# Splitting a tile's expert queries between two rounds, gathering its retrieval into fewer ticks, and gate rows by transposing a column

## What is computed

```python
for l in range(DEPTH):                                    # 2
    mod = silu(c) @ ada_w[l] + ada_b[l]                   # 6 sections of 1024
    sh_m, sc_m, g_m, sh_f, sc_f, g_f = split(mod, 6)
    h = rmsnorm(x, norm_mix_g[l]) * (1 + sc_m) + sh_m
    cols = h @ w_in[l]                                    # 1024 x 3332
    y = concat(diff_attention(cols), rwkv7(cols), forgetting_attention(cols))
    x = x + g_m * (y @ w_out[l])
    h = rmsnorm(x, norm_ffn_g[l]) * (1 + sc_f) + sh_f
    q = (h @ wq).reshape(tokens, 8 heads, 2, 128)
    s = q . subkeys                                       # 2 x 128 scores a head
    # top 16 of each half, top 16 of their 256 sums -> 16 experts of 16384 a head
    u, v = u_tab[eidx], v_tab[eidx]                       # 128 experts a token
    coef = softmax(top scores) * gelu(u . h)
    x = x + g_f * sum(coef * v)
out = rmsnorm(x, final_norm_g)
```

## Time and profile before

| | us |
|---|---|
| median of 3 runs (1898.29 to 1904.04) | 1902.0 |
| the profiled execution | 1903.03 |
| its span | 1901.2 |
| lead, to the first expert row | 290.75 |
| round 0, round 1, round 2, round 3 | 425.35, 421.2, 422.4, 325.0 |
| after the last tick | 16.5 |

### The profile page before, as it was taken

The page is one execution under the profiler, slowest core; times in us unless marked ns, Lnnn a source line. Parts: engine busy times, 40 slices in busy tenths (PEclk is TensorE's granted clock), DMA queues, the critical chain, the costliest instruction groups (busy, mean ns, idle before and its releaser), DMA issues.

```text
span 1901.2 us, 20926 instructions
## 1 busy us (share of the span) xinstructions
PE 1616.6 (85%) x6868; PEld 1006.0 (53%) x6868; DVE 1394.7 (73%) x3315; ACT 673.4 (35%) x1640; POOL 515.2 (27%) x564
## 2 busy tenths in 40 slices
PE   1767678898999998898999998898999997887776
PEld 1656665554665655564665655554665652332222
DVE  5866598997856758998765748988765759985554
ACT  1313114334732334335632235325632233331112
POOL 2000013222233232222233232222232233343331
PEclk9889788998999999998999999999999998999999
DMA  9982688997799999998999999998899999999996
GB/s 393 422 346 101 242 353 348 367 421 286 283 399 421 422 420 395 363 422 313 321 403 421 421 421 399 370 402 293 287 403 421 421 415 401 416 407 421 421 421 256
DMA packets 96989, 706.08 MB, mean 371 GB/s; under 512 B 10992, under 2 KB 11504, under 8 KB 13296
## 3 DMA queue, kind: packets, MB, share of 16 engines
q0 software_dynamic: 80640, 587.24, 77.1%
q1 hardware_dynamic: 16240, 117.50, 15.1%
HBM read 703.64 MB, written 1.05 MB: 371 GB/s over the span
## 4 chain that ended last, share of the span: by engine, by line
PE 49%; DVE 28%; DMA 16%; ACT 3%; issue 3%; POOL 0%; DVEq 0%; ACTq 0%; POOLq 0%
PE psum L772 26%; DMA ringmem<-in_peer_uv_dram,eidx 11%; DVE ringmem L1435 9%; PE psum L648 5%; PE psum L412 4%; DMA W<-in_w_groups_dram 3%; PE psum L635 2%; DMA ringmem<-in_ada_pairs_dram 2%; PE psum L520 1%; PE psum L508 1%; DVE ringmem L1079 1%; PE psum L518 1%; PE psum L415 1%; DVE coef L1448 1%; ACT diag L1050 1%
## 5 line engine op out<-in xcount | busy, mean ns | idle before, releaser
L772 PE MATMUL psum<-ringmem,diag 128*128 128x512 f32 x2048 | 978.4, 624 | 132.3 <-ACT diag L1050 132.0
L379 POOL DMA_INDIRECT ringmem<-in_peer_uv_dram,eidx x512 | 489.5, 956 | 1131.5 <-PE psum L772 1079.7
L1435 DVE SCALAR_TENSOR_TENSOR ringmem<-ringmem,psum 128x1024 f32<-128x1024 f32 x512 | 612.5, 1220 | 195.3 <-DMA ringmem<-in_peer_uv_dram,eidx 180.1
L772 PEld LDWEIGHTS psum<-ringmem,diag 128*128 128x128 f32 x2048 | 389.1, 199 | 608.1 <-issue 409.1
L1050 ACT ACTIVATE diag<-K,coef 128x128 f32<-128x128 f32 x512 | 176.4, 393 | 225.8 <-DVE coef L1448 225.6
L412 PE MATMUL psum<-hT,W 128*128 128x128 f32 x1344 | 172.3, 287 | 40.9 <-DMA W<-in_w_groups_dram 19.1
L412 PEld LDWEIGHTS psum<-hT,W 128*128 128x128 f32 x1344 | 169.2, 203 | 64.9 <-issue 38.0
L1042 ACT ACTIVATE coef<-dots 128x2 f32<-128x2 f32 x256 | 51.8, 202 | 408.6 <-DVE ringmem L1435 407.7
L1079 DVE SCALAR_TENSOR_TENSOR ringmem<-ringmem,diag 128x1024 f32<-128x1024 f32 x96 | 115.3, 1223 | 20.9 <-DMA ringmem<-in_ada_pairs_dram 18.8
L648 PEld LDWEIGHTS psum<-hT,W 128*128 128x128 f32 x1024 | 123.2, 197 | 12.8 <-issue 7.2
L648 PE MATMUL psum<-hT,W 128*128 128x128 f32 x1024 | 126.0, 281 | 3.1 <-ACT hT L821 3.0
(11 more groups left out here) (243 smaller groups left out, 1629.7 us busy)
## 6 DMA issues: line engine op xcount, KB each, us to landing
ringmem<-in_ada_pairs_dram POOLq DMA_DIRECT2D x48, 1024.0 KB, 19.0
W<-in_w_pieces_dram SPq DMA_DIRECT2D x48, 1024.0 KB, 9.2
W<-in_w_groups_dram SPq DMA_DIRECT2D x24, 1536.0 KB, 11.3
W<-in_w_groups_dram SPq DMA_DIRECT2D x12, 1024.0 KB, 9.6
ringmem<-in_peer_uv_dram,eidx POOLq DMA_INDIRECT x512, 11.7
W<-in_w_groups_dram SPq DMA_DIRECT2D x4, 1040.0 KB, 9.2
attn<-in_subkeys_t_dram SPq DMA_DIRECT2D x4, 1024.0 KB, 9.5
K<-in_consts_dram SPq DMA_DIRECT2D x1, 1546.0 KB, 18.1
```

The source lines that it names most:

```text
L379: nc.gpsimd.indirect_dma_start(slot(k), None, rows, bass.IndirectOffsetOnAxis(ap=eidx[:, ph % 2, m:m + 1], axis=0)).then_inc(row_landed[q ...
L772: mm = nc.tensor.matmul(acc[:, q], diag[:, k % DIAGS, :], slot(k)[:, D:][:, q], start=(k % SEL == 0), stop=(k % SEL == SEL - 1), skip_grou ...
L1435: ins = v.scalar_tensor_tensor(out=u, in0=u, scalar=1.0, in1=hrep, op0=ALU.mult, op1=ALU.mult, accum_out=dots[:, j:j + 1])
```

## The change

1. **The split of the queries.** The lead ends after segment 64 (`LEAD_END`), when the queries of heads 0 to 3 are done and heads 0 and 1 are found; segments 65 to 78 of mixing 0 run in the first ticks of round 0. In rounds 0 to 2 the next tile's mixing goes up to segment 70 (`MIX_END`), and its segments 71 to 78 (query of head 7, scores of heads 6 and 7) run in the first ticks of the round that follows. The next tile's mixing starts in tick 7 of round 0 and in tick 3 of rounds 1 and 2, where it was tick 1.
2. **Retrieval.** Segments 61 to 64 do two parts each instead of 61 to 68 one each. Heads 2 to 7 are found in ticks 1 to 16 (`FIND`), by turns two parts and one part a tick, where it was one part in each of ticks 0 to 23.
3. **`lead_pace`.** Pieces of `ada` per segment: 1.15 up to 28 (was 1.3), 0.9 up to 56 (was 0.5 up to 50, then 1.6), 3 up to 64.
4. **Gate rows.** TensorE transposes a column of `MC` that is read 128 times; the diagonals on ScalarE and the product with ones are gone. The row of `g_f` is made in segment 58 instead of 75 and 76.

```diff
-def pace():
-
-    total, done, out = sum(COST), 0, [-1] * TICKS
-    for n, w in enumerate(COST):
-        tick = 1 + (TICKS - 3) * done // total
-        for m in range(tick, TICKS):
-            out[m] = n
+LEAD_END, MIX_END = 65, 71
+
+
+def pace(ph):
+
+
+    first = MIX_END if ph else LEAD_END
+    todo = [(n, -1) for n in range(first, SEGMENTS)]
+    if ph + 1 < PHASES:
+        todo += [(END - 1, n) for n in range(MIX_END)]
+    else:
+        todo += [(END - 1, n) for n in (4, 6, 75, 76, 77)]
+    cost = [COST[old if new < 0 else new] for old, new in todo]
+    done, total, out = 0, max(sum(cost), 1100), [(first - 1, -1)] * TICKS
+    for (old, new), w in zip(todo, cost):
+        for m in range((TICKS - 4) * done // total, TICKS):
+            out[m] = (old, new)
         done += w
     return out
...
-    for seg in range(2, SEGMENTS):
-        due += 1.3 if seg <= 28 else 0.5 if seg <= 50 else 1.6
+    for seg in range(2, LEAD_END):
+        due += 1.15 if seg <= 28 else 0.9 if seg <= 56 else 3
         out += [seg] * (int(min(due, ADA_CHUNKS)) - len(out))
-    return out + [SEGMENTS] * (ADA_CHUNKS - len(out))
...
+FIND = [[] for _ in range(TICKS)]
+for _n in range(4 * (PH - 2)):
+    FIND[1 + 2 * _n // 3].append((2 + _n // 4, _n % 4))
...
+                        if i and seg == QRY0 + 1:
+
+                            for half in range(2):
+                                gate_row(g_at(i, 2 + half), (i - 1) // NT, G_F, half, bank[4 + half],
+                                         ("hT_dve", at("hT_dve", i, 3)))
...
-                        if i and seg == 75:
-                            gate_row(g_at(i, 2), gdiag[1], bank[6], ("q_sb", at("q_sb", i, 7)))
-                        elif i and seg == 76:
-                            gate_row(g_at(i, 3), gdiag[1], bank[6], ("g_sb", g_at(i, 3)))
-
-                def gate_row(nth, src, dst, bank_free):
-
-                    pe.wait_ge(s["g_diag"], nth + 1)
+
+                def gate_row(nth, l, section, half, dst, bank_free):
+
+                    pe.wait_ge(s["mod_ready"], 3 if l else 2)
                     pe.wait_ge(s[bank_free[0]], bank_free[1])
                     for j in range(4):
-                        mm = nc.tensor.matmul(dst[:, j * P:(j + 1) * P], ones[:], src[:, j, :], start=True, stop=True)
-                    mm.then_inc(s["g_out"], 1)
+                        k = 4 * half + j
+                        tr = nc.tensor.transpose(dst[:, j * P:(j + 1) * P],
+                                                 MC[:, l, section, k:k + 1].broadcast_to([P, P]), ident)
+                    tr.then_inc(s["g_out"], 1)
...
-                Pace(mixing(0)).upto(END - 1)
+                own = Pace(mixing(0))
+                own.upto(LEAD_END - 1)
                 place_h(0)
                 for ph in range(PHASES):
                     beside = Pace(mixing(ph + 1) if ph + 1 < PHASES else last_gate())
                     for m in range(TICKS):
-                        beside.upto(PACE[m])
+                        own.upto(PACE[ph][m][0])
+                        beside.upto(PACE[ph][m][1])
                         if m == TICKS - 1 and ph + 1 < PHASES:
                             place_h(ph + 1)
                         weigh(ph * TICKS + m)
+                    own = beside
...
-                        elif 61 <= seg <= 68:
-                            retrieve(i, (seg - 61) // 4, (seg - 61) % 4)
+                        elif 61 <= seg <= 64:
+                            for part in range(2):
+                                retrieve(i, (seg - 61) // 2, 2 * ((seg - 61) % 2) + part)
...
-                        if m < 4 * (PH - 2):
-                            retrieve(ph, 2 + m // 4, m % 4)
-                        beside.upto(PACE[m])
+                        for h, part in FIND[m]:
+                            retrieve(ph, h, part)
+                        own.upto(PACE[ph][m][0])
                         if m == 0 and ph:
                             add_sum(ph - 1)
+                        beside.upto(PACE[ph][m][1])
                         coefficients(n)
+                    own = beside
```

More of the change, by code:

```diff
@@ L150, in trunk @@
     gelu, exp, sig = ACT.Gelu, ACT.Exp, ACT.Sigmoid
-    PACE, LEAD = pace(), lead_pace()
+    PACE, LEAD = [pace(ph) for ph in range(PHASES)], lead_pace()
     with ExitStack() as ctx:
@@ L791, in gate_exp @@
                     nc.scalar.activation(e, e, exp, accum_out=gsum[:, i % 2, h:h + 1]).then_inc(s["gate_exp"], 1)
-                def gate_diag(l, section, half, dst):
-                    for j in range(4):
-                        ins = nc.scalar.activation(dst[:, j, :], ident, ACT.Copy,
-                                                   scale=MC[:, l, section, 4 * half + j:4 * half + j + 1])
-                    ins.then_inc(s["g_diag"], 1)
                 def gate_copy(nth, half, src):
```

62 lines of the change are left out of this document (30 added, 32 removed).

## The result

The changed kernel takes 1958.1 us (median of 4 runs, 1952.08 to 1963.74) against 1901.3 beside it (4 runs, 1898.29 to 1904.04): a ratio of 1.030, 95% interval 1.026 to 1.033. The forecast was 1914, with a range to 1931. The sign was right, the size was not: 57 us where 12 were forecast. The profiled execution is the fastest of the four, 1952.08 with a span of 1950.3, so its two traces differ by 49 us; the other 8 us have no trace.

What follows compares the result with a forecast made beforehand. Rounds 0 to 2 were taken as bound by VectorE, then TensorE, then transfers. Lead -3, rounds 0 and 1 0, round 2 +2, round 3 +13 sum to +12: 1903.0 becomes 1915, forecast median 1914 us, range 1892 to 1931.

Steps and rivals of the forecast that it cites:

- What bounds the kernel: Before, rounds 0 to 2: VectorE bounds ticks 0 to 23, TensorE 24 to 43, transfers 44 to 63 at 419 to 421 GB/s.
- Ticks 0 to 16: Rounds 1 and 2: VectorE is the bound throughout with retrieval, rows, mixing and waits, 136 us.
- Ticks 24 to 43: Mixing ends at segment 70, so slightly less TensorE work in rounds 1 and 2: 0, -3, -3 us for rounds 0 to 2.
- Heads 0 and 1: End of a round: finding them in three ticks costs a little of the gain in ticks 44 to 63.
- Ticks 44 to 63: Rounds 0 to 2: loads worth 6 us move past the boundary in rounds 0 and 1; -5, -3, +1 us.
- Gate rows: Less ScalarE and TensorE work on gate rows, counted as a gain of 1 us a round inside other terms.
- The lead: Before row 0: 1.59 us won at the wait for place_h and 1.4 us from the new pace, -3 us.
- Round 3: VectorE's 27 us surplus over transfers in ticks 0 to 16 exceeds the DMA ring's 7 to 12 us lead: +13, bounds +8, +17.
- A: Rival: crowding costs nothing in rounds 0 to 2, first stretches stay at 173 to 176 us; 1899 us, chance 0.20.
- B: Rival: A, plus the lead keeps all 8 us and round 3's ring lead is 12; 1889 us, chance 0.13.
- C: Rival: TensorE's clock falls and stays down behind VectorE-bound ticks 7 to 16; 1924 us, chance 0.15 together with D.
- D: Rival: queries in ticks 0 to 6 of round 0 wait for ScalarE, +7 us; 1921 us, chance 0.15 together with C.

Runs made afterwards that it cites:

- e3_split_tiles_1_3: b1_both_spread with the lead pace of before and all of mixing 0 done in the lead, only tiles 1 to 3 split: 1880.2 us.
- a1_find_spread: The changed kernel with heads 2 to 7 found one part a tick in ticks 0 to 23 again: 1903.1 us.
- a3_tail_spread: The changed kernel with heads 0 and 1 of tiles 1 to 3 found one part a segment in segments 61 to 68 again: 1939.8 us.
- b1_both_spread: The changed kernel with the spreads of both a1_find_spread and a3_tail_spread: 1884.3 us.
- e1: The kernel before, with the first two weight groups of tiles 2 and 3 loaded only after the last dot product of rounds 0 and 1: 1894.9 us.

## Why the prediction was wrong

By its steps, with the profiled executions (forecast, then measured):

| step | forecast | measured |
|---|---|---|
| lead | -3 | 0 |
| round 0 | 0 | +10.0 |
| round 1 | 0 | +10.2 |
| round 2 | +2 | +13.7 |
| round 3 | +13 | +16.8 |
| behind the last tick | 0 | -1.8 |

**What bounds the kernel** was read rightly for most of the single stretches: ticks 17-23 of rounds 1 and 2 at 42.8 and 43.2 with TensorE busy 42 (44 forecast), ticks 44-63 of rounds 0 and 1 at 123.5 and 121.2 (124 to 126), ticks 0-16 of round 3 at 115.3 with 354 GB/s (112 with 350), the rest of it at 4.8 us a tick. It was not for ticks 0-16 of rounds 1 and 2: there VectorE was to be busy over 95% with transfers under 340 GB/s, and was busy 88 and 89% with 366 and 371 GB/s.

**Ticks 0 to 16, the first step that failed.** I summed VectorE's rows, retrieval and mixing to 130 us and put 6 for the adding of the sums and the waits together. In round 1 all its work was 125, the waits 17. The work came out smaller because the 62 us for six heads were read from the length of four ticks, gaps included; VectorE's busy time in ticks 0-23 of round 3, 121.5 less 24 ticks of 2.7, leaves at most 57. Before, the same 17 ticks of round 1 had 120.5 us with 108.6 busy, 12 us of gaps that a window would have shown; I took the waits from the start of the mixing alone. Of the other 5, some 4 are in tick 0 of round 1: `place_h` comes late (4.6 us in place of 1.5), and so do the sums (1.0). Against the forecast of 136 that is 7 and 4 us too little for rounds 1 and 2.

**Ticks 24 to 43, the second and the larger.** I gave rounds 1 and 2 -3 us for "slightly less of TensorE's work", after I had already set ticks 17-23 at TensorE's own sum of 44. Both together make 160 us for round 1 and 164 for round 2, and TensorE was busy 160.0 and 167.6 in them. So I had forecast stretches without a single wait, where the earlier trace rows show 2 to 3% of waits in ticks 24 to 43; they took 167.5 and 174.1. Round 0 missed in both directions: counted from the first dot product, ticks 0-23 went down from 171.4 to 164.3 us where I had +5, and ticks 24-43 went up from 121.9 to 146.0 where I had 0. The queries in ticks 0-6 and a mixing that starts in tick 7 push TensorE's work back, 138.7 us of it into ticks 24-43, which had 119.0; I had moved none. e3_split_tiles_1_3 shows the packed mixing to be worth 11.5 us of the round.

**The crowding taken by itself** was put at 5 + 6 + 4 + 13 = 28 us. a1_find_spread puts it at 6.4, 13.6, 12.9 and 17.4 in the traces, 50, and at 55 by the medians.

**Heads 0 and 1** were given "a little" inside the term for ticks 44-63. a3_tail_spread and b1_both_spread put them at 18 to 19 us. That was the term with no working of its own, and the worst. That ticks 44-63 still came out near the forecast is luck: without this crowding they are 119.2, 116.7 and 118.5 us in b1_both_spread, 11, 12 and 5 under the kernel before, where I had counted on 5 and 3 less and 1 more. A gain that I had put too small hid a cost that I had put too small.

**Ticks 44 to 63**, the loads past the boundary: 6 us forecast, 7.3 and 7.7 measured alone (e1). Right. **Gate rows**: 1 us a round forecast, 0 to -4 in all measured. **The lead**: the 1.59 us for `place_h` went as forecast, and as much was lost ahead of it.

**Round 3** stands at the upper bound of its term, +17, with a surplus that the ring did not hide, as argued.

**Rivals.** A and B are out: ticks 0-16 of rounds 0 to 2 grew by 15 to 22 us and round 3 by 17. C as I priced it is out: in ticks 17-23, behind the stretch with the waits, the granted clock is 1.00, which is 2.4 GHz. The rule of the Trainium skill that I weighed ("TensorE: Matmul & The Clock Gate", section "HAM oscillation — how this bites in real kernels") is seen in single rows: the weighing that waited 4.70 us above took 5.91 at a granted clock of 0.62, where its like takes 3.60. The clock did fall in the crowded stretch itself, and weighing is busy 16.5 us longer than in a1_find_spread; so the clock can have a part in the 55 us of the crowding, which no run separates. D is out: ticks 0-7 of round 0 took 50.3 us, less than the 54.4 before.

So the measured sum is: 55 us for heads 2 to 7, 18 for heads 0 and 1, 0 to 4 for gate rows, and by difference -16 to -20 for the split and the paces, of which the late loads, measured on the kernel before, are -7.5. My terms for that last group added up to -16, so the whole miss is in the two crowdings, 28 us and "a little" forecast against 55 and 18.
